# Reading the high half of f32 expert weights in place, instead of splitting off a bf16 copy

## The reference

```python
g_idx = top_1(softmax(h @ rg_w + rg_b))              # 4 groups
e_idx = top_2(softmax(expert logits of that group))   # 8 experts per group, 32 in all
# tokens are sorted by expert and padded to blocks of 128 rows
def expert_block(xb, e):
    return (silu(xb @ w_gate[e]) * (xb @ w_up[e])) @ w_down[e]
# w_gate, w_up: 1024 x 512; w_down: 512 x 1024; all float32
y = sum over a token's two experts of weight * expert_block(...)
```

## Time and profile before

| | |
|---|---|
| time of the profiled execution | 3012.16 us |
| its span, first to last instruction | 3010.3 us |
| median of the runs | 3012.16 us |
| PE busy | 2693.3 us (89%) |
| DVE busy | 1582.9 us (53%) |
| POOL busy | 1288.7 us (43%) |
| ACT busy | 807.7 us (27%) |
| DVE casts of the weights (L841) | 93, 232.3 us in all, 2498 ns each |
| DVE subtractions of the weights (L843) | 93, 426.6 us in all, 4587 ns each |
| POOL subtractions in the router (L945) | 3, 25.4 us in all |

### The profile page before, as it was taken

One profiled execution on the slowest core, in us unless ns is written; L12 is line 12 of the kernel. 1 busy time (PEld: TensorE's weight loads), 2 busy tenths in 40 slices (PEclk: granted clock), 3 DMA queues, 4 the chain that ended last, 5 costly groups with the idle time before them and its releaser, 6 DMA issues. The chain is left out here.

```text
span 3010.3 us, 45887 instructions
## 1 busy us (share of the span) xinstructions
PE 2693.3 (89%) x15218; PEld 1454.7 (48%) x15503; DVE 1582.9 (53%) x1909; ACT 807.7 (27%) x1109; POOL 1288.7 (43%) x1031
## 2 busy tenths in 40 slices
PE   5999999999999999993399999999999999999900
PEld 2555555555555555552244444444444444444400
DVE  6455445554445554446955634544433454654268
ACT  4221122221222221222033333333333333233322
POOL 0111111111111111113468855766665766775569
PEclk9999999999999999996699999999999999999955
DMA  6001011100011100004367765766765767766266
GB/s 250 29 36 42 28 42 42 42 35 37 33 42 42 42 35 35 28 28 168 101 232 249 231 175 168 227 201 208 225 180 149 224 203 226 247 209 179 57 216 244
DMA packets 144542, 390.21 MB, mean 130 GB/s; under 512 B 15872, under 2 KB 18288, under 8 KB 143488
## 3 DMA queue, kind: packets, MB, share of 16 engines
q1 hardware_dynamic: 114336, 287.85, 27.4%
q0 software_dynamic: 25568, 85.20, 12.2%
q10 hardware_dynamic: 4608, 16.78, 1.4%
HBM read 296.45 MB, written 93.34 MB: 129 GB/s over the span
## 5 line engine op out<-in xcount | busy, mean ns | idle before, releaser
L841 DVE CAST w_high<-w_stage 128x4096 bf16<-128x4096 f32 x93 | 232.3, 2498 | 665.2 <-PE ebank L1298 664.9
L1297 PE MATMUL ebank<-w_low,x_t 128*128 x1262 | 479.4, 380 | 2.3 <-issue 0.2
L1296 PE MATMUL ebank<-w_high,x_t 128*128 x1223 | 464.6, 380 | 2.0
L1298 PE MATMUL ebank<-w_high,x_t 128*128 x1226 | 465.7, 380 | 0.1
L843 DVE TENSOR_TENSOR w_low<-w_stage,w_high 128x4096 bf16<-128x4096 f32 x93 | 426.6, 4587 | 3.2
L350 POOL TENSOR_TENSOR rstd<-moments,eps 128x1 f32<-128x1 f32 x65 | 12.3, 189 | 936.6 <-DVE moments L503 936.6
L666 PE MATMUL bank<-w_in,h_t 128*128 128x512 f16 x1024 | 389.4, 380 | 5.1 <-issue 0.2
L665 PE MATMUL bank<-w_in,h_t 128*128 128x512 bf16 x930 | 353.7, 380 | 7.1 <-DMA router_b_sb<-in_re_b 7.1
L1297 PE MATMUL ebank<-w_low,hid_t 128*128 x632 | 240.2, 380 | 2.0
L668 PE MATMUL bank<-w_in,h_t 128*128 128x512 bf16 x1024 | 241.9, 379 | 0.0
L1296 PE MATMUL ebank<-w_high,hid_t 128*128 x594 | 225.9, 380 | 4.0 <-ACT hid_t L1234 2.0
(11 more groups left out here) (217 smaller groups left out, 4404.3 us busy)
## 6 DMA issues: line engine op xcount, KB each, us to landing
w_stage<-in_w_gate SPq DMA_DIRECT2D x32, 2048.0 KB, 9.4
w_stage<-in_w_up SPq DMA_DIRECT2D x32, 2048.0 KB
w_stage<-in_w_down SPq DMA_DIRECT2D x32, 2048.0 KB
x_in<-in_x SPq DMA_DIRECT2D x32, 512.0 KB, 3.3
h_dram<-stage SPq DMA_DIRECT2D x32, 512.0 KB, 2.6
parts_dram<-stage SPq DMA_DIRECT2D x32, 512.0 KB, 2.6
h_back<-h_dram SPq DMA_DIRECT2D x32, 512.0 KB, 5.3
out<-h_back ACTq DMA_DIRECT2D x32, 512.0 KB, 3.7
```

Source lines behind the costliest of these rows:

```text
L841: engine.tensor_copy(hi, raw).then_inc(w["high"], 1)
L1296: nc.tensor.matmul(dst, lhs(0, k), hi(k), start=k == 0, stop=False)
L1297: nc.tensor.matmul(dst, lhs(0, k), lo(k), start=False, stop=False)
L1298: ins = nc.tensor.matmul(dst, lhs(1, k), hi(k), start=False, stop=k == kts - 1)
```

## The change

The f32 weights are loaded into two full slots (`raw`, one per expert in turn) and stay there while the expert is used. A bf16 number has the layout of the upper 16 bits of an f32, so the high half is no longer made: `hi` is the same memory seen as bf16, and the matmuls of the high passes read every second element of it, beginning with element 1. The high half is therefore the f32 cut off rather than rounded, and the low half is the f32 minus that, as before in bf16. Only the subtraction is left of the splitting; `w_high`, ScalarE's casts in the router and VectorE's casts in the experts are gone. The memory is the same: 96 KB per partition for `w_stage` and `w_high` before, 96 KB for `raw` now.

A load now writes into the slot that the matmuls read, so it is SP that waits for TensorE to be done with expert e-2, part by part, and VectorE waits only for the load. The loads of the second expert move ahead on SP's queue in the router.

```diff
--- before.py
+++ after.py
@@ -808,39 +808,35 @@
 def weight_slots(nc, ctx):
 
     m = Memory(nc, ctx)
+    raw = m.sb("raw", [P, 2 * SLOT], F32)
     return {
-        "stage": m.sb("w_stage", [P, 3, PART], F32),
-        "hi": m.sb("w_high", [P, 2 * SLOT], BF16),
+        "raw": raw, "hi": raw[:].bitcast(BF16),
         "lo": m.sb("w_low", [P, 2 * SLOT], BF16),
         "ident": [m.sb(f"ident_{q}", [P, P], dt) for q, dt in enumerate((BF16, F16))],
-        "loaded": [m.sem(f"w_loaded{j}") for j in range(3)],
-        "high": m.sem("w_high_made"),
+        "loaded": [[m.sem(f"w_loaded{i}{j}") for j in range(3)] for i in range(2)],
         "low": m.sem("w_low_made"),
     }
 
 
-def load_expert(eng, a, w, e):
+def load_expert(eng, a, w, e, free=None):
 
     sources = (("w_gate", D_E), ("w_up", D_E), ("w_down", D))
     for part, (name, width) in enumerate(sources):
-        if not (isinstance(e.i, int) and e.n < 1):
-            eng.wait_ge(w["low"], 3 * e.n + (part - 2))
+        at = e.slot * SLOT + part * PART
+        if free is not None:
+            eng.wait_ge(free[0][part], free[1])
         src = a[name].rearrange("e (k p) n -> e p k n", p=P)[bass.ds(e.n, 1), :, :, :].squeeze(0)
-        eng.dma_start(w["stage"][:, part, :].rearrange("p (k n) -> p k n", n=width),
-                      src).then_inc(w["loaded"][part], 16)
-
-
-def split_parts(dve, engine, w, e, free=None):
+        eng.dma_start(w["raw"][:, at:at + PART].rearrange("p (k n) -> p k n", n=width),
+                      src).then_inc(w["loaded"][e.slot][part], 16)
+
+
+def low_parts(eng, engine, w, slot, count):
 
     for part in range(3):
-        at = e.slot * SLOT + part * PART
-        dve.wait_ge(w["loaded"][part], 16 * e.n + 16)
-        if free is not None:
-            dve.wait_ge(free[0][part], free[1])
-        hi, raw = w["hi"][:, at:at + PART], w["stage"][:, part, :]
-        engine.tensor_copy(hi, raw).then_inc(w["high"], 1)
-        dve.wait_ge(w["high"], 3 * e.n + (part + 1))
-        engine.tensor_tensor(w["lo"][:, at:at + PART], raw, hi, ALU.subtract).then_inc(w["low"], 1)
+        at = slot * SLOT + part * PART
+        eng.wait_ge(w["loaded"][slot][part], 16 * count)
+        engine.tensor_tensor(w["lo"][:, at:at + PART], w["raw"][:, at:at + PART],
+                             w["hi"][:, 2 * at + 1:2 * (at + PART):2], ALU.subtract).then_inc(w["low"], 1)
 
 
 def router(nc, a, keep, w):
@@ -911,6 +907,7 @@
             sp.dma_start(before[:], a["before"]).then_inc(loaded, 16)
             sp.dma_start(ident_f[:], a["ident"]).then_inc(id_loaded, 16)
             load_expert(sp, a, w, Tile(0, 0))
+            load_expert(sp, a, w, Tile(0, 1))
             for name in ("ln2_g", "ln2_b"):
                 sp.dma_start(keep[name][:], a[name].partition_broadcast(P)).then_inc(ln2_loaded, 16)
 
@@ -919,7 +916,6 @@
             sp.dma_start(keep["h1_dram"][spares, :], zeros[:]).then_inc(rows_stored, 16)
             sp.dma_start(keep["parts_dram"][spares, :], zeros[:].bitcast(BF16)).then_inc(rows_stored, 16)
             sp.dma_start(keep["weights_dram"][spares, :], zeros[:, 0:EXPERTS]).then_inc(rows_stored, 16)
-            load_expert(sp, a, w, Tile(0, 1))
             sp.wait_ge(weights_made, 1)
             sp.dma_start(keep["weights_dram"][0:SEQ, :].rearrange("(t p) e -> p t e", p=P), rank[:]).then_inc(rows_stored, 16)
             sp.wait_ge(rows_stored, 16 * 4)
@@ -939,11 +935,7 @@
             nc.gpsimd.iota(number[:], pattern=[[0, 1]], base=0, channel_multiplier=1,
                            allow_small_or_imprecise_dtypes=True).then_inc(made, 1)
             nc.gpsimd.memset(keep_going[:], 1.0).then_inc(made, 1)
-            for part in range(3):
-                cols = slice(part * PART, (part + 1) * PART)
-                pool.wait_ge(w["high"], part + 1)
-                nc.gpsimd.tensor_tensor(w["lo"][:, cols], w["stage"][:, part, :], w["hi"][:, cols],
-                                        ALU.subtract).then_inc(w["low"], 1)
+            low_parts(pool, nc.gpsimd, w, 0, 1)
 
             pool.wait_ge(made, 7)
             pool.wait_ge(places, 1)
@@ -1082,10 +1074,6 @@
 
         @block.scalar
         def _(act):
-            for part in range(3):
-                act.wait_ge(w["loaded"][part], 16)
-                nc.scalar.activation(w["hi"][:, part * PART:(part + 1) * PART], w["stage"][:, part, :],
-                                     ACT.Copy).then_inc(w["high"], 1)
             act.wait_ge(step, mark["g_shifted"])
             nc.scalar.activation(g_exp[:], g_exp[:], ACT.Exp).then_inc(act_step, 1)
             act.wait_ge(step, mark["ratio"])
@@ -1159,17 +1147,18 @@
         def _(sp):
             with sp.Fori(0, EXPERTS // 2 - 1) as i:
                 for k in range(2):
-                    load_expert(sp, a, w, Tile(i, 2 + k))
+                    e = Tile(i, 2 + k)
+
+                    end = sp.value_load(keep["ends"][0:1, bass.ds((e - 2).n, 1)], min_val=1, max_val=BLOCKS)
+                    load_expert(sp, a, w, e, ([s["gate"], s["up"], s["down"]], end))
 
         @block.vector
         def _(dve):
 
-            split_parts(dve, nc.vector, w, Tile(0, 1))
-            with dve.Fori(0, EXPERTS // 2 - 1) as i:
-                for k in range(2):
-                    e = Tile(i, 2 + k)
-                    end = dve.value_load(keep["ends"][0:1, bass.ds((e - 2).n, 1)], min_val=1, max_val=BLOCKS)
-                    split_parts(dve, nc.vector, w, e, ([s["gate"], s["up"], s["down"]], end))
+            low_parts(dve, nc.vector, w, 1, 1)
+            with dve.Fori(1, EXPERTS // 2) as i:
+                for slot in range(2):
+                    low_parts(dve, nc.vector, w, slot, i + 1)
 
         @block.gpsimd
         def _(pool):
@@ -1290,7 +1279,7 @@
                 ins.then_inc(s["xtr"], 1)
 
             def passes(dst, lhs, at, stride, kts, done):
-                hi = lambda k: w_hi[:, bass.ds(at + k * stride, BANK)]
+                hi = lambda k: w_hi[:, bass.ds(at * 2 + (2 * k * stride + 1), BANK, step=2)]
                 lo = lambda k: w_lo[:, bass.ds(at + k * stride, BANK)]
                 for k in range(kts):
                     nc.tensor.matmul(dst, lhs(0, k), hi(k), start=k == 0, stop=False)
```

## The result

| kernel | median, us | runs from, to | ratio to before |
|---|---|---|---|
| before | 3012.69 | 3011.93 to 3016.6 | 1 |
| after | 3039.53 | 3034.94 to 3041.3 (4) | 1.0087 [1.0073, 1.0101] |

The change makes the kernel 0.9% slower, where 2985 us was forecast. The range, 2976 to 3012, missed it. The profiled execution spans 3034.5 us against 3010.3 before, so there are +24.2 us to explain.

A forecast was written before the change was run, and what follows sets the result against it. TensorE was taken to bound the expert stage and VectorE's chain the router. From 3012.16 us, -19.6 (disturbance) - 6.9 (start) - 0.5 (router) = -27.0 gave 2985 us, range 2976 to 3012.

The forecast's parts named there:

- strided read: High-half matmuls in the expert blocks, 3792 reading at a 4-byte step: taken as 0 us, against +857 at half rate.
- disturbance in the blocks: Expert blocks: TensorE's waits for hidden rows and gathers go once VectorE's casts stop locking GpSimd, -19.6 us.
- start of the experts: Start of the expert stage: second gather issued between subtractions, landing at 1499.8 against 1506.74, -6.9 us.
- router: Router: GpSimd's low parts start earlier without ScalarE's cast, VectorE's chain ends at 1438.1 against 1438.66, -0.5 us.
- loads: Weight loads waiting on SP for expert e-2's products: 14.7 us slack at the tightest, 0 us.
- Rival (a): Expert blocks: the strided operand halves the rate of the high passes, 3842 us; chance 0.15.
- The argument on one measured block: Expert blocks: new order laid on one measured block; GpSimd's hidden-row work at most one subtraction, 4.4 us, late.
- The alternative that the prediction had worked out: Start of the experts: if the subtraction also stopped the gather's issue, the second gather lands at 1507.6, +0.9 us.
- no weight wait on TensorE: Expert stage: loads were to arrive in time; weight waits appearing on TensorE would have shown the forecast wrong.

The follow-up runs named there:

- e3: Separate program without the layer: TensorE alone runs 48 matmuls of each kind, columns read at different steps; 275.72 us in all.
- e1: Changed kernel with the high passes reading contiguous columns of w_low instead of every second element of raw; 3003.12 us, 0.9956 of before.
- e2: Kernel before with the high passes reading w_high's even columns, then odd ones, at a 4-byte step, casts kept; 3043.05 us, 1.0094 of before.
- e5: Kernel before, first expert's subtractions moved from GpSimd to VectorE behind the first gather, second expert's loads later, ScalarE's exponentials moved ahead among its casts; 2998.11 us, 0.9946.
- e4: Kernel before, first expert's three subtractions moved from GpSimd in the router to VectorE at the expert stage's start, second expert's loads also later; 3004.4 us, 0.9964.

## Why the prediction was wrong, step by step

| step | forecast, us | measured, us |
|---|---|---|
| strided read | 0 | +35.7 |
| disturbance in the blocks | -19.6 | -8.0 |
| start of the experts | -6.9 | -0.6 |
| router | -0.5 | -3.7 |
| loads | 0 | 0 |
| tail | - | -1.1 |

The start and the router are measured from the first weight load's issue, 1401.24 after and 1399.32 before; this offset of +1.9 lies in the mixer, which the change leaves alone, and within the 5 us by which it differs between executions. With it: 35.7 - 8.0 - 0.6 - 3.7 - 1.1 + 1.9 = +24.2, as the spans have it. "Router" runs to the end of VectorE's "both", "start" from there to the first activation, "tail" from the last activation to the end.

**The strided read is the step that failed**, and it alone turns the sign. The prediction weighed 0 against +857 us and took 0, by the row it was nearest to. No run shows that 0: e3 has 226 ns for 216 at a step of 2, and the layer took 35.7 us for it. That the doubling of the f32 matmuls is not a matter of bytes fits e3's figure: their 128 columns of 4 bytes touch 32 times 16 bytes, an estimated 56 ns beneath the 110 of the earlier trace rows. No run tests f32 itself. What did not follow is that a 16-bit operand in steps is free. Rival (a) had the kind, a limit in bytes, and its threshold, "over 7 ns more than its 216", was the right one: the cost was 9.6 ns. But it was given only one size, the halved rate, and 0.15. Between 0 and +857 lay a whole range of prices, of which all but the lowest 3% make the kernel slower. With even weight over that range slower would have been the likelier side; no row showed such an operand, and none gave a reason for exactly 0.

**The disturbance: -8.0 of -19.6.** The prediction let the subtractions be late by at most one, and let gather issues pass. Both fail at expert 24, the expert with one block, and that place holds most of what is left. VectorE's and GpSimd's timeline there in the changed kernel:

```profile
2595.44 4.42 DVE L838 TENSOR_TENSOR w_low<-raw 128x4096 bf16<-128x4096 f32 x1 [1.72 <-DMA raw<-in_w_gate]
2595.60 5.29 POOL L1201 TENSOR_TENSOR hid_parts<-hid,hid_parts 128x512 f16<-128x512 f32 x1 [0.74 <-ACT hid_parts L1255]
2600.87 4.43 DVE L838 TENSOR_TENSOR w_low<-raw 128x4096 bf16<-128x4096 f32 x1 [1.00 <-DMA raw<-in_w_up]
2601.84 4.33 POOL L1175 DMA_INDIRECT xg<-parts_dram,index  x1 [0.82 <-POOL index L1167]
2605.98 4.43 DVE L838 TENSOR_TENSOR w_low<-raw 128x4096 bf16<-128x4096 f32 x1 [0.69 <-DMA raw<-in_w_down]
2606.18 4.27 POOL L1167 COPY y_index<-tokens 128x1 uint32 x1
2612.68 4.42 DVE L838 TENSOR_TENSOR w_low<-raw 128x4096 bf16<-128x4096 f32 x1 [2.27 <-DMA raw<-in_w_gate]
2620.44 4.42 DVE L838 TENSOR_TENSOR w_low<-raw 128x4096 bf16<-128x4096 f32 x1 [3.33 <-DMA raw<-in_w_up]
2620.99 4.89 POOL L1201 TENSOR_TENSOR hid_parts<-hid,hid_parts 128x512 f16<-128x512 f32 x1 [0.74 <-ACT hid_parts L1255]
2625.93 1.03 PE L1311 MATMUL htr<-ident,hid_parts 128*128 128x128 bf16 x8 [7.16 <-POOL hid_parts L1201]
```

Each subtraction starts when a load lands and is 4.4 us long, and each one has caught a GpSimd operation, a copy of one element (4.27) or an issue (4.33) as much as a 512-wide one. Six loads, two experts' worth, land within 31 us here, and six locks in 36 us (the first starts at 2589.30) leave GpSimd late enough that TensorE waits 7.16 us. The two blocks around it take 22.97 and 21.99 us; over 17.34 each that is 10.3 of the 11.6 left. Most of what the wait does not explain is the granted clock, which fell from 1.00 to 0.50 while TensorE stood still. The stretch behind the wait (columns of the earlier trace rows) and two strided matmuls in it:

```profile
2626.00:2630.00 4.00, 4.00 (x16) 1.93 (x17) 0.00 (x0) 1.09 (x2) 2.33 (x5) 0.50 0.37 117
2627.62 0.63 PE L1287 MATMUL ebank<-raw,x_t 128*128 x1
2628.05 0.63 PE L1285 MATMUL ebank<-raw,x_t 128*128 x1
```

At the granted clock of 0.50 ten matmuls stand 0.43 us apart instead of 0.22 (2.1 us) and the transposes take 1.03 us instead of 0.62.

The prediction quoted 2.60 us of wait for this place, which is too little. Before, TensorE waited there three times (1.66, 2.60 and 2.75 us, the last with the granted clock at 0.50 behind it, from 2608 to 2610), and three intervals of 18.93, 23.96 and 17.01 us were 9.3 over 3 x 16.88. So nearly half of the 19.6 stood at the one place that the new order was not laid out for, and it has grown by about 1. All of the gain was made in the other blocks. There the waits did go: the wait for hidden rows, 9.7 us in 14 pieces before, has 0.7 us left outside this place. Not all of the -8.0 need be the casts: e1, with blocks of the old length, has 7.4 us less disturbance than before, but e2, with longer blocks and all casts, has 6.0 less too. The argument on one measured block was right for experts with several blocks, and was not laid out for the one where the next expert's loads come together.

**The start: -0.6 of -6.9.** The subtraction does stop the gather's issue. VectorE and GpSimd after:

```profile
1488.11 13.12 DVE L838 TENSOR_TENSOR w_low<-raw 128x4096 bf16<-128x4096 f32 x3 [0.30 <-PEq L845]
1489.30 4.39 POOL L1175 DMA_INDIRECT xg<-parts_dram,index  x1 [1.01 <-issue]
1493.71 3.24 POOL L1167 COPY index<-tokens 128x1 uint32<-128x1 uint32 x1
1497.78 4.29 POOL L1175 DMA_INDIRECT xg<-parts_dram,index  x1 [0.84 <-POOL index L1167]
1505.23 1.89 PE L1278 MATMUL xtr<-ident,xg 128*128 128x128 bf16 x16 [6.15 <-DMA xg<-parts_dram,index]
```

Three subtractions are one row here. The issues take 4.39 and 4.29 us, against 0.96 at the shortest, and the three subtractions, 4.37 each, end at about 1492.5, 1496.9 and 1501.2. The prediction read 1.1 us of an issue inside a subtraction in the earlier trace rows as proof that the two go together. It showed only that an issue under way is let finish, not that one that arrives inside may begin. The two issues here end about 1 us behind the end of a subtraction, the copy at the end of one. The alternative that the prediction had worked out, +0.9 us, is close to what came: from the end of the router's "both" to the second transposes it is 68.4 us, for 68.1 before. The -0.6 of the table comes behind them, by a cause that the prediction did not name: at a granted clock of 0.50 matmuls are 0.43 us apart until 1508.2 after and until 1511.7 before, about five matmuls more before, or 1.1 us.

**The router: -3.7 of -0.5.** VectorE and GpSimd after, to be laid against the earlier trace rows:

```profile
1411.10 21.48 POOL L838 TENSOR_TENSOR w_low<-raw 128x4096 bf16<-128x4096 f32 x3 [8.13 <-DMA raw<-in_w_gate]
1411.90 6.66 DVE L962 TENSOR_TENSOR cand<-prod,best 128x256 f32<-128x256 f32 x1
1418.60 7.12 DVE L964 SCALAR_TENSOR_TENSOR cand<-cand,iota 128x256 f32<-128x256 f32 x1
1425.75 0.42 DVE L966 TENSOR_REDUCE place<-cand 128x32 f32<-128x256 f32 x1
1426.20 6.43 DVE L986 TENSOR_TENSOR ratio<-best 128x32 f32<-128x32 f32 x1
1435.64 1.22 DVE L992 TENSOR_TENSOR both<-member 128x1024 f16<-128x1024 f32 x1
```

The strict turns came as forecast, three operations held 6.4 to 7.1 us each. The mis-sized term is the part's length: the prediction had parts of 7.7 us with turns of 0.4 between them, 23.9 us in all, and it was 21.48 with the turns (7.18 a part), so no cost of the 4-byte step shows on GpSimd. That is 2.4 of the 3.2 us. GpSimd started 9.9 us behind the first weight load, not 9.1 (+0.7), and so met VectorE further along: 4.3 us of chain were left behind its last part, not 5.7 (-1.4).

**Right** were: no weight wait on TensorE; subtractions of 4.43 us at a load's landing, unslowed on VectorE (4410/4426/5365 ns over 93); VectorE's freed 236 us worth nothing in themselves.

## What to carry to other kernels

An operand that a bound engine reads 3792 times must be priced before anything else: 10 ns on each outweighed all that the removed work gave, and where no row shows the form of the operand, a short loop of matmuls at steps 1 and 2 settles it (e3). Work on an engine off the path is worth only the locks and waits it causes; count these per place, and lay the argument out for the odd case (here the expert with one block), not for the regular one. What is gained at a start is handed on only if the work put off does not land on the blocks behind it (e5: 30.3 us gained, 13.3 given back). And a time from the start of one execution is compared with another only from a common event: here stages that no edit touched moved everything behind them by up to 5 us.

## What the runs showed of the hardware

- TensorE's moving operand: 512 16-bit columns take 216, 226, 340, 451, 900 and 918 ns at steps of 1, 2, 3, 4, 8 and 16 elements, as if each 16 bytes touched took 1.76 ns (an estimate; step 1 lies above it). The pitch at step 8 was the same, 0.90 us, at a granted clock of 1.00 and of 0.50; only its first matmuls ran at 1.00, the rest and all of step 16 at 0.50. In the layer, too, step 2 costs 10 ns at 1.00 and nothing that shows at 0.50, where strided and contiguous matmuls both stand 0.43 us apart. In e3 the granted clock fell at step 8, after TensorE had started only one matmul every 0.9 us (stretches of e3: length, busy time of TensorE's matmuls and weight loads, two idle engines, granted clock, DMA share, GB/s):

```profile
152.00:154.00 2.00, 2.00 (x4) 0.24 (x2) 0.00 (x0) 0.00 (x0) 1.00 0.00 0
156.00:160.00 4.00, 4.00 (x6) 0.53 (x5) 0.00 (x0) 0.00 (x0) 0.50 0.00 0
```

- An indirect DMA's issue on GpSimd that arrived during a two-input subtraction of VectorE waited for its end: 4.3 to 4.4 us for 1.0 (the changed kernel, e4, e5). A reduction on VectorE (0.42 us at 1425.75) was not held by GpSimd's subtraction (the third, 7.2 us from 1425.4).
